# One hybrid decoder layer on one core: another order for the output gates' blocks, and four pieces of side work moved by a step or more

## The chip, the cores and the metric

The kernel runs on one core of a Trainium2 chip. The metric is the device time of one execution in microseconds (us). The kernel before takes 1752.5 us (median of 3 runs, 1751.62 to 1753.2).

## The reference, cut to what matters

```python
h = _rmsnorm(x, norm_gain)                      # x: 256 tokens of 4096 columns, float32
proj = h @ w_in                                 # one combined input projection
(m_q, m_k, m_v, m_o, m_z, m_i, m_f, a_q, ...) = jnp.split(proj, split_points, axis=-1)
qk = jax.nn.silu(_causal_conv(jnp.concatenate([m_q, m_k], axis=-1), w_conv))
...
h_m = _mlstm(mq, mk, mv, i_pre, f_pre)          # 4 heads: scores, decay, numerator / denominator
h_m = jax.nn.sigmoid(m_o) * h_m                 # output gate
h_m = h_m * lax.rsqrt(jnp.mean(h_m * h_m, axis=-1, keepdims=True) + RMS_EPS) * mlstm_norm_gain
y_m = h_m * jax.nn.silu(m_z)                    # second gate
y_a = _nsa(...) * jax.nn.silu(a_z)              # sparse attention, 16 heads
mix = jnp.concatenate([y_m, y_a], axis=-1)
x = x + mix @ w_out
return _rmsnorm(x, final_norm_gain)
```

The change touches the part with the four mLSTM heads and nothing of what is computed.

## The kernel before, in words

**Matmuls.** The weights come as a stream of pairs, each 2 x 128 rows of 512 output columns. A 32-bit product is made of three passes (lines 721 to 723): high half by high half, and each high half by the other's low half. ScalarE (ACT) makes the high half of a pair (line 1253), VectorE (DVE) the low half (line 1775), both three steps ahead of TensorE (PE), in a ring of four slots. A step of the stream is one pair for all 256 tokens: 2 token tiles x 2 x 3 = 12 matmuls.

**Twos.** For some column blocks two blocks are done at once (class `Two`, `two`). Of a pair of blocks some row pairs ("quads") are done in the plain way, one step for each block: an *eight*. The others are done together by a Strassen-like scheme with 7 products in place of 8: a *seven*, which takes the place of two steps and has 21 matmuls. A seven needs sums of weights: DVE makes them in `m_t_raw` (line 2047, then 2052 and 2062), ACT makes their high halves in `m_t_hi` (line 1403 for the first two sums, line 1410 for the other two), DVE their low halves in `m_t_lo` (lines 2057 and 2067). There is one set of these tiles. So the ACT instruction on line 1403 waits for the semaphore `t_used`, which PE raises with the last matmul of the seven before. On PE a seven runs in this order: six matmuls on the plain weights (into `bank_xy` and `acc_a`), six on the first two sums (they wait for `t13_lo`), three on plain weights (into `acc_b`), six on the other two sums (they wait for `t24_lo`, from line 2067).

**Heads.** Each head h of the mLSTM has a block of gates (output gate m_o and second gate m_z as one Two, order `ORDER_M`: 6 sevens and 10 pairs of eights, 32 steps) and, but for the last head, a block of keys (queries and keys of the next head as one column block and its values as the other: 4 sevens, at steps 4, 8, 12 and 16). Heads 0 to 2 run in a hardware loop, and the gates of head 3 stand behind it. They are followed by the first block of the output projection.

**Side work by step.** Each engine's program carries side work by the step's number: scores of the head (`SCORES`), numerators and denominators (`NUMERATOR`, on PE; DVE's `normalise` one step later), sums of the shared and own banks of a Two at its end (`SUMS_GATES`, `shared_products`, `own_products`, lines 2081 and 2087), which free the accumulators `acc_a` and `acc_b` for the next block. In the keys' block: the output gate, the second gate and `head_output` (line 2309) at the three numbers of `PRODUCTS_KEYS`, the scaling of queries and keys on ACT (`key_scale`, line 1612), and at step `CONV_KEYS` PE transposes them (line 763) for the convolution. In the gates of head 3 eight further pieces turn the attention's output into the next left operand: `mix_hi` on ACT (line 1313), `mix_lo` on DVE (line 1845), at the steps of `MIX_TAIL`.

The order within a two is a list of (row pair, block). A Two's `few` says whether a row pair is a quad of the seven kind, `last(h)` in which step block h gets its last product. DVE adds block 0's accumulators when that step's `pe_used` is there.

Of the kernel before, what the change touches and what calls it, by code (L numbers as in the profile page):

```python
# [89 lines left out]
MIX_TAIL, MIX_TURN = 24, 1  # L90
# [10 lines left out]
ORDER_M = (6, 7, 8, 0, 9, 1, 10, 2, 11, 3, 12, 4, 13, 5, 14, 15)  # L101
# [7 lines left out]
def interleaved(order):  # L109

    return tuple((c, h) for c in order for h in range(2))

# [63 lines left out]
PRODUCTS_KEYS, PRODUCTS_LAST = (2, 6, 10), (1, 4, 5)  # L176
SCORES, NUMERATOR = 0, 3
SUMS_GATES, SUMS_KEYS = 28, 18
CONV_V, CONV_KEYS = 1, 22
# [47 lines left out]
def hybrid_layer(nc, x, x_cols_first, w_all, final_norm_gain,  # L227
                 consts, early_consts, toe_bias, s_lo_kept, out):
    ctx = ExitStack()
    with ctx:  # L230
# [208 lines left out]
        def gates_two(h):  # L439

            return Two(4 * h * PAIRS + M0, 2 * h + 1, per_head * h + len(SEVEN), len(SEVEN),
                       interleaved(ORDER_M), (acc[0], acc[1]), [bx, by, bz, bv],
                       (kv_s_hi, m_s_lo), (m_t_hi, m_t_lo, m_t_raw))
# [785 lines left out]
        def _(act):  # L1229
# [319 lines left out]
            def head_pieces(h):  # L1549
# [93 lines left out]
                return two_pieces, conv_at, gates_at, (SUMS_KEYS, key_product), (CONV_KEYS - 1, key_scale)  # L1643
# [24 lines left out]
            gates(HEADS_M - 1, {MIX_TAIL + c: [lambda c=c: mix_hi(c)] for c in range(MIX_M)})  # L1668
# [83 lines left out]
        def _(dve):  # L1752
# [471 lines left out]
            def head_pieces(h):  # L2224
# [72 lines left out]
                def sums_at(w, c, last):  # L2297
                    return (*[(c + part // 2, lambda part=part: shared_products(w, m_shared, part))
                              for part in range(4)], (last, lambda: own_sums(w, 0)))
# [18 lines left out]
                def gates_at(o, z, y):  # L2318
# [6 lines left out]
                              *sums_at(gates_two(h), SUMS_GATES, SUMS_GATES + 3))  # L2325
# [5 lines left out]
            def keys(h):  # L2331
                _, _, gates_at, sums_at, own_sums = head_pieces(h)
                two_stream(keys_two(h), piece_map(
                    *gates_at(*PRODUCTS_KEYS), *sums_at(keys_two(h), SUMS_KEYS, CONV_KEYS - 2),
                    *head_pieces(h + 1)[1](CONV_KEYS)))
                own_sums(keys_two(h), 1)
# [24 lines left out]
            gates(HEADS_M - 1, [(MIX_TAIL + c, lambda c=c: mix_lo(c)) for c in range(MIX_M)])  # L2361
# [234 lines left out]
def weight_stream(w_in, w_out, cmp_k_w1, cmp_v_w1):  # L2596
# [37 lines left out]
    for h in range(HEADS_M):  # L2634
        gates = [block(w_in, run(col + h * BW)) for col in (C_MO, C_MZ)]
        pairs += [gates[i][c] for c, i in interleaved(ORDER_M)]
        if h < HEADS_M - 1:
            blocks = keys(h + 1)
            pairs += [blocks[i][c] for c, i in keys_first(FEW_V)]
# [41 lines left out]
```

## Time and profile before

| | us |
|---|---|
| median of 3 runs | 1752.5 |
| the profiled execution | 1752.96 |
| its span, first to last instruction | 1751.2 |
| PE busy | 1733.5 (99%) |
| DVE busy | 1313.6 (75%) |
| ACT busy | 947.6 (54%) |

In the trace the stretch of the four heads runs from about 788 to 1401 us. Start times are from the span's start. A PE row's duration is that of one matmul through a pipelined array (0.39 us), while the next one starts well before it ends, so idle time in brackets counts only what lies behind that end.

### The profile page before, as it was taken

Reading aid. Unit: us, or ns where it says so; the run is one execution under the profiler, and the core shown is the slowest. Engines: PE = TensorE matmul, PEld = TensorE weight load, DVE = VectorE, ACT = ScalarE, POOL = GpSimd, SP = SyncE. Lnnn points to the kernel's source line nnn. Section 1 sums busy time; section 2 is a strip of 40 time slices with the busy share of each in tenths; the row PEclk is TensorE's granted clock in tenths of the full one; section 3 lists DMA queues with packets and bytes.
Section 4 is the critical chain, followed back from the end, with each engine's and each line's share of the span. In section 5 each row is a group of like instructions: output and inputs, shape, how many; then the busy total and the mean of one; then the engine's idle time right before and its main releaser. Section 6 shows DMA issues by size and latency. Waiting matters only on the chain.

```text
span 1751.2 us, 23455 instructions
## 1 busy us (share of the span) xinstructions
PE 1733.5 (99%) x8000; PEld 1437.0 (82%) x8000; DVE 1313.6 (75%) x1679; ACT 947.6 (54%) x1318; POOL 20.0 (1%) x33
## 2 busy tenths in 40 slices
PE   9999999999999999999999999999999999999997
PEld 7888888888888888888888888888888788888886
DVE  7556786566675756668887888788878988888876
ACT  7535555455555555545555555555555665564553
POOL 0000000000000000000000000000000000000000
PEclk9999999999999999999999999999999999999999
DMA  9657656545455454555646564666565656666674
GB/s 383 241 179 234 214 195 221 185 157 183 154 188 170 158 182 161 174 181 204 216 169 217 205 215 169 217 206 212 174 213 208 206 187 212 216 217 215 217 262 182
DMA packets 98325, 354.59 MB, mean 202 GB/s; under 512 B 10688, under 2 KB 11200, under 8 KB 97472
## 3 DMA queue, kind: packets, MB, share of 16 engines
q1 hardware_dynamic: 94480, 336.96, 55.7%
q10 hardware_dynamic: 3760, 16.52, 2.7%
q8 instruction: 51, 0.84, 0.2%
q14 instruction: 34, 0.28, 0.1%
HBM read 347.67 MB, written 5.77 MB: 202 GB/s over the span
## 4 chain that ended last, share of the span: by engine, by line
PE 88%; DVE 5%; DMA 3%; issue 2%; ACT 1%; SPq 0%; DVEq 0%; POOLq 0%; ACTq 0%; POOL 0%
PE acc_a L721 12%; PE acc_a L723 12%; PE acc_a L722 12%; PE acc_b L721 11%; PE acc_b L723 11%; PE acc_b L722 11%; DMA w_raw<-in_w_all 3%; PE bank_xy L721 3%; PE bank_xy L722 3%; PE bank_xy L723 3%; PE bank_z L723 1%; PE bank_z L721 1%; PE bank_z L722 1%; PE bank_v L722 1%; PE bank_v L723 1%
## 5 line engine op out<-in xcount | busy, mean ns | idle before, releaser
L1775 DVE TENSOR_TENSOR w_split<-w_raw,w_split 128x1024 fp32r<-128x1024 f32 x495 | 599.5, 1222 | 263.0 <-ACT w_split L1253 254.3
L1253 ACT ACTIVATE w_split<-w_raw 128x1024 fp32r<-128x1024 f32 x494 | 518.1, 1056 | 366.1 <-PE acc_b L723 176.8
L721 PE MATMUL acc_a<-w_split,lhs_hi 128*128 128x512 f32 x968 | 379.9, 392 | 2.6 <-DVE stage L2087 2.4
L723 PE MATMUL acc_a<-w_split,lhs_lo 128*128 128x512 f32 x968 | 377.2, 390 | 0.0
L722 PE MATMUL acc_a<-w_split,lhs_hi 128*128 128x512 f32 x968 | 377.2, 390 | 0.0
L721 PE MATMUL acc_b<-w_split,lhs_hi 128*128 128x512 f32 x890 | 348.4, 391 | 0.0
L723 PE MATMUL acc_b<-w_split,lhs_lo 128*128 128x512 f32 x890 | 346.6, 389 | 0.0
L722 PE MATMUL acc_b<-w_split,lhs_hi 128*128 128x512 f32 x890 | 346.5, 389 | 0.0
L721 PEld LDWEIGHTS acc_a<-w_split,lhs_hi 128*128 128x128 f32 x968 | 181.8, 188 | 39.6 <-issue 2.5
L723 PEld LDWEIGHTS acc_a<-w_split,lhs_lo 128*128 128x128 f32 x968 | 181.7, 188 | 38.5
L722 PEld LDWEIGHTS acc_a<-w_split,lhs_hi 128*128 128x128 f32 x968 | 181.9, 188 | 33.8
L723 PEld LDWEIGHTS acc_b<-w_split,lhs_lo 128*128 128x128 f32 x890 | 167.1, 188 | 35.1
L722 PEld LDWEIGHTS acc_b<-w_split,lhs_hi 128*128 128x128 f32 x890 | 167.2, 188 | 33.4
L721 PEld LDWEIGHTS acc_b<-w_split,lhs_hi 128*128 128x128 f32 x890 | 167.1, 188 | 33.2
L2038 DVE TENSOR_TENSOR w_split<-w_raw,w_split 128x1024 fp32r<-128x1024 f32 x120 | 114.2, 951 | 3.5 <-ACT w_split L1397 2.0
L1397 ACT ACTIVATE w_split<-w_raw 128x1024 fp32r<-128x1024 f32 x60 | 63.7, 1062 | 32.7 <-PE acc_a L723 16.7
L1403 ACT ACTIVATE m_t_hi<-m_t_raw 128x1024 fp32r<-128x1024 f32 x36 | 38.2, 1061 | 72.9 <-PE bank_z L723 40.5
L1410 ACT ACTIVATE m_t_hi<-m_t_raw 128x1024 fp32r<-128x1024 f32 x36 | 38.2, 1060 | 56.2 <-DVE m_t_raw L2062 56.2
L2067 DVE TENSOR_TENSOR m_t_lo<-m_t_raw,m_t_hi 128x1024 fp32r<-128x1024 f32 x36 | 44.1, 1226 | 17.9 <-ACT m_t_hi L1410 17.9
L2162 DVE TENSOR_TENSOR pt_lo<-bank_z,pt_hi 128x512 fp32r<-128x512 f32 (+1 forms) x32 | 17.9, 558 | 49.5 <-ACT pct L1487 49.5
L2047 DVE TENSOR_TENSOR m_t_raw<-w_raw 128x1024 f32<-128x1024 f32 x36 | 44.0, 1222 | 11.4 <-DMA w_raw<-in_w_all 7.4
L1485 ACT ACTIVATE pt_hi<-bank_z 128x512 fp32r<-128x512 f32 (+1 forms) x32 | 15.7, 491 | 66.8 <-PE bank_v L1067 66.8
(457 smaller groups left out, 2142.2 us busy)
## 6 DMA issues: line engine op xcount, KB each, us to landing
w_raw<-in_w_all SPq DMA_DIRECT2D x614, 512.0 KB
m_s_lo<-s_lo_kept ACTq DMA_DIRECT2D x4, 1536.0 KB, 7.5
wide<-in_x SPq DMA_DIRECT2D x8, 512.0 KB, 10.3
xres<-in_x ACTq DMA_DIRECT2D x8, 512.0 KB, 5.7
out_y<-wide SPq DMA_DIRECT2D x8, 512.0 KB, 3.6
gained_x<-in_x_cols_first SPq DMA_DIRECT2D x6, 512.0 KB, 7.5
toe<-in_toe_bias ACTq DMA_DIRECT2D x4, 512.0 KB, 5.0
gain_f<-in_final_norm_gain ACTq DMA_DIRECT2D x1, 2048.0 KB, 9.9
```

What stands on the lines that cost most here:

```text
L721: pe.matmul(dst, a[0], b[0], start=start, stop=False)
L722: pe.matmul(dst, a[0], b[1], start=False, stop=False)
L723: return pe.matmul(dst, a[1], b[0], start=False, stop=stop)
L1253: act.activation(w_hi[:, cols], w_raw[:, cols], ACT.Copy).then_inc(hi_done, 1)
L1397: act.activation(w_hi[:, cols], w_raw[:, cols], ACT.Copy).then_inc(hi_done, 1)
L1403: act.activation(sum_hi[:, 0:2 * BW], sum_raw[:, 0:2 * BW], ACT.Copy).then_inc(t13_hi, 1)
L1410: act.activation(sum_hi[:, 2 * BW:].rearrange("p (i c) -> p i c", i=2), sum_raw[:, :].rearrange("p (i c) -> p i c", i=3)[:, 0:3:2, :], ACT ...
L1775: dve.tensor_tensor(w_lo[:, cols], w_raw[:, cols], w_hi[:, cols].bitcast(F32), ALU.subtract).then_inc(lo_done, 1)
L2038: return dve.tensor_tensor(w_lo[:, cols], w_raw[:, cols], w_hi[:, cols].bitcast(F32), ALU.subtract)
L2047: dve.tensor_tensor(sums[:, 0:2, :], tile(1, 0, 2).rearrange("p (i c) -> p i c", i=2), w_raw[:, 2 * s * BW:(2 * s + 4) * BW].rearrange("p ...
L2067: dve.tensor_tensor(sum_lo[:, 2 * BW:].rearrange("p (i c) -> p i c", i=2), sums[:, 0:3:2, :], sum_hi[:, 2 * BW:].bitcast(F32).rearrange("p ...
L2162: dve.tensor_tensor(in_batch(pt_lo, u), transposed_tiles(u), in_batch(pt_hi, u).bitcast(F32), ALU.subtract)
```

## The change

The gates' order `ORDER_M` begins with row pairs 6, 7, 8, 9 (all of them eights), and then 0 and 1 (both sevens) follow each other; 0 stood between 8 and 9 before. A new function, `gates_in_turn`, makes the last two row pairs (14, 15) run for block 0 first and then for block 1, so block 0 (the output gate) gets its last product at step 29 and not 30. Its own sums move from step 31 to 30. The numerators move from step 3 to 4 (and `normalise` with them from 4 to 5). In the keys' block the transposes and the convolution behind them move from 22 to 23, while own sums and key scale stay at 20 and 21; `head_output` moves from step 10 to 15, and DVE waits for it before the shared sums. `MIX_TAIL` spreads the eight mix pieces: steps 24 to 31 before, 10, 14, 18, 22, 26, 28, 31, 31 now.

```diff
@@ -87,7 +87,7 @@
 
 
 MIX_EARLY, MIX_LATE = PAIRS - 2, 11
-MIX_TAIL, MIX_TURN = 24, 1
+MIX_TAIL, MIX_TURN = (10, 14, 18, 22, 26, 28, 31, 31), 1
 
 MIX_M = PAIRS // 2
 
@@ -98,7 +98,7 @@
 TWOS = 3
 SEVEN = tuple(range(6))
 ORDER = (6, 7, 0, 8, 1, 9, 2, 10, 3, 11, 4, 12, 5, 13, 14, 15)
-ORDER_M = (6, 7, 8, 0, 9, 1, 10, 2, 11, 3, 12, 4, 13, 5, 14, 15)
+ORDER_M = (6, 7, 8, 9, 0, 1, 10, 2, 11, 3, 12, 4, 13, 5, 14, 15)
 FEW_V = 4
 S1, S2, S3, S4 = range(4)
 SUM_ORDER, SUMS = (S1, S3, S2, S4), 5
@@ -109,6 +109,12 @@
 def interleaved(order):
 
     return tuple((c, h) for c in order for h in range(2))
+
+
+def gates_in_turn(order):
+
+    last = order[-2:]
+    return interleaved(order[:-2]) + tuple((c, h) for h in range(2) for c in last)
 
 
 def keys_first(quads):
@@ -173,10 +179,11 @@
 
 
 GATES_KEYS, GATES_LAST = (0, 3, 4), (0, 2, 3)
-PRODUCTS_KEYS, PRODUCTS_LAST = (2, 6, 10), (1, 4, 5)
-SCORES, NUMERATOR = 0, 3
+PRODUCTS_KEYS, PRODUCTS_LAST = (2, 6, 15), (1, 4, 5)
+SCORES, NUMERATOR = 0, 4
 SUMS_GATES, SUMS_KEYS = 28, 18
-CONV_V, CONV_KEYS = 1, 22
+CONV_V, CONV_KEYS = 1, 23
+OWN_KEYS = 20
 RESIDUAL = 12
 
 WARM = 8
@@ -439,7 +446,7 @@
         def gates_two(h):
 
             return Two(4 * h * PAIRS + M0, 2 * h + 1, per_head * h + len(SEVEN), len(SEVEN),
-                       interleaved(ORDER_M), (acc[0], acc[1]), [bx, by, bz, bv],
+                       gates_in_turn(ORDER_M), (acc[0], acc[1]), [bx, by, bz, bv],
                        (kv_s_hi, m_s_lo), (m_t_hi, m_t_lo, m_t_raw))
 
         def keys_two(h):
@@ -1640,7 +1647,7 @@
 
                 two_pieces = piece_map((0, values_hi), (SCORES, input_sums_lo), (SCORES + 1, sw_hi_part),
                                        (SUMS_GATES, gate_product))
-                return two_pieces, conv_at, gates_at, (SUMS_KEYS, key_product), (CONV_KEYS - 1, key_scale)
+                return two_pieces, conv_at, gates_at, (SUMS_KEYS, key_product), (OWN_KEYS + 1, key_scale)
 
             def gates(h, late={}, behind=None):
                 found = head_pieces(h)[0]
@@ -1665,7 +1672,7 @@
                 act.wait_ge(s_raw_done, SUM_ORDER.index(f) + 1)
                 act.activation(s_hi[:, f], s_raw[:, f], ACT.Copy).then_inc(s_hi_done, 1)
 
-            gates(HEADS_M - 1, {MIX_TAIL + c: [lambda c=c: mix_hi(c)] for c in range(MIX_M)})
+            gates(HEADS_M - 1, piece_map(*[(MIX_TAIL[c], lambda c=c: mix_hi(c)) for c in range(MIX_M)]))
             last_gates = piece_map(*head_pieces(HEADS_M - 1)[2](*GATES_LAST))
 
 
@@ -2322,7 +2329,7 @@
                 two_pieces = ((SCORES, scores), (SCORES + 1, values_lo), (SCORES + 2, scores_lo),
                               (NUMERATOR + 1, lambda: normalise(0)),
                               (NUMERATOR + 1, lambda: normalise(1)),
-                              *sums_at(gates_two(h), SUMS_GATES, SUMS_GATES + 3))
+                              *sums_at(gates_two(h), SUMS_GATES, SUMS_GATES + 2))
                 return two_pieces, conv_at, gates_at, sums_at, own_sums
 
             def gates(h, late=(), behind=None):
@@ -2331,7 +2338,8 @@
             def keys(h):
                 _, _, gates_at, sums_at, own_sums = head_pieces(h)
                 two_stream(keys_two(h), piece_map(
-                    *gates_at(*PRODUCTS_KEYS), *sums_at(keys_two(h), SUMS_KEYS, CONV_KEYS - 2),
+                    *gates_at(*PRODUCTS_KEYS), (SUMS_KEYS, lambda: dve.wait_ge(ym_done, h + 1)),
+                    *sums_at(keys_two(h), SUMS_KEYS, OWN_KEYS),
                     *head_pieces(h + 1)[1](CONV_KEYS)))
                 own_sums(keys_two(h), 1)
 
@@ -2358,7 +2366,7 @@
                 if f == SUM_ORDER[-1]:
                     last.then_inc(s_lo_done, 1)
 
-            gates(HEADS_M - 1, [(MIX_TAIL + c, lambda c=c: mix_lo(c)) for c in range(MIX_M)])
+            gates(HEADS_M - 1, [(MIX_TAIL[c], lambda c=c: mix_lo(c)) for c in range(MIX_M)])
             late = piece_map(*head_pieces(HEADS_M - 1)[2](*PRODUCTS_LAST))
             for i, f in enumerate(SUM_ORDER):
                 late.setdefault(SUMS + i, []).append(lambda f=f: input_sum(f))
@@ -2633,7 +2641,7 @@
     pairs += sum(keys(0), [])
     for h in range(HEADS_M):
         gates = [block(w_in, run(col + h * BW)) for col in (C_MO, C_MZ)]
-        pairs += [gates[i][c] for c, i in interleaved(ORDER_M)]
+        pairs += [gates[i][c] for c, i in gates_in_turn(ORDER_M)]
         if h < HEADS_M - 1:
             blocks = keys(h + 1)
             pairs += [blocks[i][c] for c, i in keys_first(FEW_V)]
```

Two places of the order. On **ACT**, in the loop's block of gates, the rows from the first seven's second high half (line 1410, in the changed kernel 1417) to the next seven's first (line 1403, then 1410). Before:

```order
L1410 ACTIVATE m_t_hi<-m_t_raw 128x1024 [waits lo_done]
L1247 REGISTER_ALU
L1248 REGISTER_ALU [waits pe_used]
L1253 ACTIVATE w_split<-w_raw 128x1024 [waits w_loaded0]
L1247 REGISTER_ALU
L1253 ACTIVATE w_split<-w_raw 128x1024 [waits w_loaded1,pe_used]
L1397 ACTIVATE w_split<-w_raw 128x1024 [waits w_loaded2,pe_used]
L1398 REGISTER_ALU
L1403 ACTIVATE m_t_hi<-m_t_raw 128x1024 [waits t_used,t13_raw]
```

Now:

```order
L1410 ACTIVATE m_t_hi<-m_t_raw 128x1024 [waits t_used]
L1411 REGISTER_ALU
L1414 ACTIVATE w_split<-w_raw 128x512 [waits w_loaded1,pe_used]
L1416 REGISTER_ALU
L1417 ACTIVATE m_t_hi<-m_t_raw 128x1024 [waits lo_done]
L1401 REGISTER_ALU
L1404 ACTIVATE w_split<-w_raw 128x1024 [waits w_loaded2,pe_used]
L1405 REGISTER_ALU
L1410 ACTIVATE m_t_hi<-m_t_raw 128x1024 [waits t_used,t13_raw]
```

The two plain splits on line 1253 that stood between the sevens are gone from here; the second seven's first high half comes two instructions behind the first seven's last, and still waits for `t_used`.

On **DVE**, in the gates of head 3, the rows from the last shared sum (line 2081, then 2088) to past the own sums of block 0 (line 2087, then 2094). Before:

```order
L2081 TENSOR_TENSOR m_gate<-bank_xy,m_gate 128x512
L1845 TENSOR_TENSOR lhs_lo<-wide,lhs_hi 128x512
L1775 TENSOR_TENSOR w_split<-w_raw,w_split 128x1024
L1845 TENSOR_TENSOR lhs_lo<-wide,lhs_hi 128x512
L1775 TENSOR_TENSOR w_split<-w_raw,w_split 128x1024
L2087 TENSOR_TENSOR stage<-acc_a,stage 128x512 x2
L1845 TENSOR_TENSOR lhs_lo<-wide,lhs_hi 128x512
L1775 TENSOR_TENSOR w_split<-w_raw,w_split 128x1024
```

Now:

```order
L2088 TENSOR_TENSOR m_gate<-bank_xy,m_gate 128x512
L1782 TENSOR_TENSOR w_split<-w_raw,w_split 128x1024
L2094 TENSOR_TENSOR stage<-acc_a,stage 128x512 x2
L1782 TENSOR_TENSOR w_split<-w_raw,w_split 128x1024
L1852 TENSOR_TENSOR lhs_lo<-wide,lhs_hi 128x512 x2
L1782 TENSOR_TENSOR w_split<-w_raw,w_split 128x1024
```

The own sums of block 0 have moved ahead of one plain split (line 1775, then 1782), and two low halves of the mix (line 1845, then 1852) that stood ahead of them now stand behind them or earlier in the block.

## Rows read from the trace of the kernel before

**Rows 1.** The page: busy time (us, share, instructions) and TensorE's granted clock, tenths.

```profile
PE 1733.5 (99%) x8000; PEld 1437.0 (82%) x8000; DVE 1313.6 (75%) x1679; ACT 947.6 (54%) x1318; POOL 20.0 (1%) x33
...
PEclk9999999999999999999999999999999999999999
```

**Rows 2.** Waits of PE over the whole span: us in total, times, longest.

```profile
PE acc_a L721 <- DVE stage L2087: 2.4, 4, 1.6
PE bank_xy L721 <- DVE sw_lo L2262: 1.6, 4, 0.6
...
PE bank_v L763 <- ACT stage L1612: 1.1, 2, 0.6
```

**Rows 3.** Timeline of PE, head 0: start, duration, instruction, [idle before].

```profile
797.29 0.39 PE L723 MATMUL acc_a<-w_split,lhs_lo 128*128 128x512 f32 x1
797.91 0.49 PE L721 MATMUL bank_xy<-mv_hi,sw_hi 128*128 128x512 f32 x1 [0.24 <-DVE sw_lo L2262]
798.24 0.39 PE L722 MATMUL bank_xy<-mv_lo,sw_hi 128*128 128x512 f32 x1
```

**Rows 4.** Timeline of PE, head 0, from a seven's end to the next step.

```profile
844.33 0.39 PE L721 MATMUL acc_a<-w_split,lhs_hi 128*128 128x512 f32 x1
...
847.05 0.39 PE L721 MATMUL acc_b<-w_split,lhs_hi 128*128 128x512 f32 x1
```

**Rows 5.** Timeline of ACT, the same stretch.

```profile
844.59 1.07 ACT L1403 ACTIVATE m_t_hi<-m_t_raw 128x1024 fp32r<-128x1024 f32 x1 [2.39 <-PE bank_z L723]
...
847.67 1.06 ACT L1410 ACTIVATE m_t_hi<-m_t_raw 128x1024 fp32r<-128x1024 f32 x1 [1.50 <-DVE m_t_raw L2062]
```

**Rows 6.** Timeline of DVE, the same stretch, one seven and two eights.

```profile
842.57 1.23 DVE L2047 TENSOR_TENSOR m_t_raw<-w_raw 128x1024 f32<-128x1024 f32 x1 [0.48 <-DMA w_raw<-in_w_all]
...
845.69 1.23 DVE L2057 TENSOR_TENSOR m_t_lo<-m_t_raw,m_t_hi 128x1024 fp32r<-128x1024 f32 x1
846.95 0.69 DVE L2062 TENSOR_TENSOR m_t_raw<-w_raw,m_t_raw 128x512 f32<-128x512 f32 x1
...
848.77 1.23 DVE L2067 TENSOR_TENSOR m_t_lo<-m_t_raw,m_t_hi 128x1024 fp32r<-128x1024 f32 x1 [0.53 <-ACT m_t_hi L1410]
849.91 2.38 DVE L1775 TENSOR_TENSOR w_split<-w_raw,w_split 128x1024 fp32r<-128x1024 f32 x2
```

**Rows 7.** Timeline of DVE, head 0, first and last row of normalise.

```profile
806.49 0.15 DVE L2269 COPY den<-bank_v 128x2 f32<-128x2 f32 x1
...
808.02 0.74 DVE L2275 TENSOR_SCALAR hm<-bank_z,den 128x512 f32<-128x512 f32 x1
```

**Rows 8.** Timeline of DVE, keys behind head 0.

```profile
909.75 1.41 DVE L2309 SCALAR_TENSOR_TENSOR wide<-hm,hr,m_gate 128x512 f32 x2
911.08 2.35 DVE L1775 TENSOR_TENSOR w_split<-w_raw,w_split 128x1024 fp32r<-128x1024 f32 x2
```

**Rows 9.** Timeline of PE, the same stretch.

```profile
912.05 0.39 PE L723 MATMUL bank_z<-m_t_hi,m_s_lo 128*128 128x512 f32 x1
912.35 0.50 PE L721 MATMUL acc_a<-w_split,lhs_hi 128*128 128x512 f32 x1
```

**Rows 10.** Timeline of DVE, end of the gates of head 0.

```profile
874.18 1.23 DVE L1775 TENSOR_TENSOR w_split<-w_raw,w_split 128x1024 fp32r<-128x1024 f32 x1 [1.50 <-ACT w_split L1253]
875.32 1.28 DVE L2087 TENSOR_TENSOR stage<-acc_a,stage 128x512 f32<-128x512 f32 x2
```

**Rows 11.** Timeline of ACT, keys behind head 0, the key scale.

```profile
932.45 1.34 ACT L1612 ACTIVATE stage<-stage,rstd 128x512 f32<-128x512 f32 x2 [0.26 <-DVE stage L2087]
```

**Rows 12.** Timeline of PE, start of the output projection.

```profile
1400.92 0.47 PE L721 MATMUL acc_a<-w_split,lhs_hi 128*128 128x512 f32 x1 [1.56 <-DVE stage L2087]
```

**Rows 13.** Timeline of DVE, end of the gates of head 3.

```profile
1398.36 0.68 DVE L1845 TENSOR_TENSOR lhs_lo<-wide,lhs_hi 128x512 fp32r<-128x512 f32 x1
```

**Rows 14.** Timeline of DVE, gates of head 3, a wait for weights.

```profile
1351.16 0.69 DVE L2038 TENSOR_TENSOR w_split<-w_raw,w_split 128x512 fp32r<-128x512 f32 x1
...
1356.89 1.22 DVE L2047 TENSOR_TENSOR m_t_raw<-w_raw 128x1024 f32<-128x1024 f32 x1 [1.02 <-issue]
```

## The prediction
> **What bounds the kernel now.** I read the page first: PE is busy 1733.5 of 1751.2 us, 99%, and its granted clock shows 9 tenths or more in all 40 slices [rows 1]. So PE is the bound, and a change of order can only move the short stretches in which PE waits. The steps of PE give the scale: one plain step of 12 matmuls runs from 844.33 to 847.05, 2.72 us, one matmul every 0.227 us [rows 4]. A seven has 21 matmuls, 4.76 us.
>
> The second view was the list of PE's waits [rows 2]. Its idle time counts from a matmul's modelled end, 0.39 us after its start, while the next one normally starts after 0.227. So each wait costs its idle time and 0.16 us. Head 0 shows it: starts at 797.29 and 797.91, 0.62 us apart with 0.24 us in brackets, so 0.40 us are lost. The next matmul comes at 798.24, 0.33 later and not 0.227: a start after a wait costs 0.10 us more [rows 3].
>
> The third view was the timeline of the three engines around each of those waits and through one seven with its two plain steps [rows 4 to 6].
>
> **What goes.** Four waits, all in the heads' stretch.
>
> (1) Numerators wait for `sw_lo`: 1.6 us in 4 waits [rows 2], with 4 x 0.16 and 4 x 0.10 that is 2.6 us. One step later PE comes 2.72 us later than the longest of them (0.6 us of idle time) needs. All 2.6 us go.
>
> (2) Start of a keys' block (3 times) and of the output projection (once): 2.4 us in 4 waits for the own sums, the last one 1.56 [rows 2, 12]. With 4 x 0.16 and 4 x 0.10: 3.4 us. Before, the own sums start at 875.32, right behind the split of step 34 (874.18), which itself idled 1.50 us for ACT [rows 10]. They now stand ahead of that split and wait only for step 29, which is two steps old. They can run in that idle time and end about 1.7 us before PE needs the banks. In head 3 the eight low halves of the mix (0.68 us each [rows 13]) no longer crowd in there either. All 3.4 us go.
>
> (3) Transposes of the keys wait for ACT's key scale: 1.1 us in 2 waits [rows 2], and a third, shorter one that the list does not name. With 0.16 each I take 1.6 us. The scale's two rows end at 932.45 + 1.34 = 933.79 [rows 11], 0.4 us before PE's transposes. Own sums and scale stay at their steps and PE comes a step, 2.72 us, later. All of it goes, with over 2 us to spare.
>
> (4) In a keys' block `head_output`, 1.41 us, stands ahead of the split that PE needs next: the split (1.22 us from 911.08) ends at 912.30, PE starts at 912.35, 0.30 after its last matmul [rows 8, 9]. With the slow restart 0.18 us, 3 times: 0.5 us. At step 15 the piece stands behind the last seven, where DVE has 2.72 us for each 1.22 us split. The added wait on `ym_done` is for DVE's own product: queued behind it are the shared sums, and it costs the latency of one result.
>
> Sum of gains: 2.6 + 3.4 + 1.6 + 0.5 = 8.1 us.
>
> **What comes: two sevens side by side.** Today no matmul of a seven waits. But ACT's first high half does: at 844.59 it ends an idle time of 2.39 us, released by PE's last matmul of the seven before [rows 5], since there is one set of sum tiles. PE's next step had begun at 844.33, which I call E. From there the chain is fixed:
> - ACT line 1403 starts at E + 0.26 [rows 4, 5];
> - DVE line 2057 runs from 845.69 and ends at 846.92, E + 2.59 [rows 6];
> - line 2062 and then ACT line 1410 follow (847.67 to 848.73), and DVE line 2067 ends at 848.77 + 1.23 = 850.00, E + 5.67 [rows 5, 6].
>
> Before, two plain steps of 5.44 us lie between E and the next seven, which needs the first pair of sums 1.36 us after its start (E + 6.80) and the second 3.40 us after it (E + 8.84). Both are there. With two sevens side by side the second starts at E. It does its six plain matmuls and needs the first sums at E + 1.36, but has them at E + 2.69 (0.10 us for the signal). With the slow restart, nine matmuls end at E + 4.83. It needs the second sums then and gets them at E + 5.77. Six matmuls and the restart: it ends at E + 7.24. Without waiting it would end at E + 4.76. Loss 2.48 us, in each of four gates' blocks: 9.9 us. No other work fills this time, since PE's program is in order.
>
> **Is the second seven's other work ready?** Between the two sevens DVE now does normalise, 806.49 to 808.76, 2.27 us [rows 7], then the second seven's raw sums. The first seven sits two plain steps later than before, so DVE's part of it ends about 1.3 us before PE reaches it. Normalise then ends about 0.5 us before PE needs `hm_done`, and the raw sums and first low half fit with some 0.9 us. I cost this at nothing; if that cover fails, a few tenths per head.
>
> **Behind the pair.** The next seven's raw sums need the weights of two steps, fetched once the slots are free, that is after the split on line 2038. In head 3 that split ends at 1351.85 and the raw sums start at 1356.89: 5.04 us, the last 1.02 idle [rows 14]. In head 0 the idle time is 0.48 [rows 6], so the wait is about 4.5 us. From the raw sums to the end of line 2067 it is 7.4 us (842.57 to 850.00). The split ends at E + 3.9 in the pair's second seven, so the second low halves of the next seven are there at E + 3.9 + 4.5 + 7.4 = E + 15.8; PE needs them at E + 7.24 + 5.44 + 3.40 = E + 16.08. With 5.04 us they are 0.3 us late. From there on a cycle needs 5.6 + 4.5 = 10.1 us on this chain (weights, sums, splits) against PE's 10.20: it holds. With 5.04 it needs 10.6 and loses 0.4 us in each of the three cycles left. Before, DVE entered these cycles with a lead of 2 to 3 us, and the drift was hidden; the pair uses that lead up. So a block loses between nothing and 0.3 + 3 x 0.4 + four restarts = 1.9 us more. I take 1.2 us in all, nearly all in head 3, where the 5.04 was seen; the bounds are 0 and 7.6. The mix pieces in head 3 fall into DVE's idle time before the raw sums if the wait is there.
>
> **Sum.** -8.1 + 9.9 + 1.2 = +3.0 us. The profiled execution took 1752.96 us (span 1751.2 and 1.8 around it), so 1755.9 for that one; against the median of 1752.5 I forecast 1755.3, taking 0.2 us off for small gains not listed.
>
> **Two rules of the Trainium skill.** PE never idles at a seven today, while ACT waits for the one tile set [rows 5]. The Trainium skill, page Perfetto Trace Analysis, section Optimization Strategy, says that a gap which repeats on the engine that should be saturated can mean too few buffers. By today's PE rows alone the pair would be free (-6.9 us in all); by the rule it is the 9.9 us gap. The chain above bears the rule out.
>
> The granted clock stayed at its upper level, 2.4 GHz, through the longest wait, 1.56 us [rows 1, 12]. The page TensorE: Matmul & The Clock Gate of the Trainium skill, Part 1, says that a TensorE that idles falls to half the clock. The trace shows no fall after a wait of that length, and the pair's waits are 1.3 and 0.9 us.
>
> **The rivals.**
> - *A, the forecast:* pair loses 2.5 us a head, gains real, little drift. 1750.5 to 1756.0, chance 0.51 with what lies within 0.2%.
> - *B, slower:* the same, but the drift behind the pair appears in more than one head. It decides once the weights take over 4.76 us (E + 16.08 less 7.4 and 3.9). All four heads: -8.1 + 9.9 + 7.6 = +9.4, 1761.9; two heads: about 1758. For it: 1.02 us of idle time before the raw sums in head 3. Against: 0.48 in head 0. Chance 0.34.
> - *C, faster:* the pair costs little, because the second sums, or both, are ready in a way that I overlook. With only the first wait (1.3 + 0.1 a head) -8.1 + 5.7 = -2.4; with none -8.1, 1744.4. Against it: `t_used` still stands before the second seven's first high half. Chance 0.13, for what ends more than 3.5 us below; the -2.4 would still lie within.
> - *D:* the clock falls in the pair's waits. A step at half clock takes 2.72 us more; four steps a head would be +43 us. Against it: rows 1. Chance 0.01.
> - *E, the change does not do what it says:* normalise, now squeezed between sevens, delays PE at `hm_done` by more than 0.5 us a head; +2 us on top of A, about 1757. Chance 0.01.
>
> **Chances and range.** A measurement tells about 0.2% apart, 3.5 us. Faster than that: C, 0.13. Within: 0.51. Slower: B, D, E, 0.36. The range for 8 in 10 leaves out the better part of C and the far end of B: 1750.0 to 1760.0.
>
> **What would show it.** In the changed profile: the waits for `sw_lo`, for the own sums on line 2094 and for line 1619's scale gone; in each gates' block a wait of PE for `m_t_lo` of line 2064 with idle time about 1.2 us and one for line 2074 of 0.8. Rows of line 2074 ending later than 3.4 us after a seven's start would be B. I am wrong at the root if PE runs the second seven of the pair in 4.8 us.

## The result and the profile after

| | before | after |
|---|---|---|
| median | 1751.93 us (1751.23 to 1755.08, 19 runs) | 1755.12 us (1754.54 to 1756.44, 19 runs) |
| the profiled execution | 1752.96 | 1755.31 |
| its span | 1751.2 | 1753.5 |

The ratio is 1.0017, with a 95% interval of 1.001 to 1.0024. The change costs 3.2 us by the medians and 2.3 us by the two profiled executions; the forecast was 1755.3.

The page of the changed kernel, busy time and granted clock. It answers to [rows 1].

```profile
PE 1734.4 (99%) x8000; PEld 1437.5 (82%) x8000; DVE 1311.5 (75%) x1679; ACT 945.0 (54%) x1318; POOL 20.1 (1%) x33
...
PEclk9999999999999999999999999999999999999999
```

The work is the same and the clock is the same. What differs is where PE waits. The list of PE's waits in the changed kernel (us in total, times, longest), which answers to [rows 2]. All lines of the kernel have moved down by 7.

```profile
PE bank_xy L728 <- DVE m_t_lo L2064: 4.4, 4, 1.1
PE acc_a L728 <- DVE m_t_lo L2074: 3.1, 5, 0.7
```

The waits for `sw_lo`, for the own sums and for the key scale are gone, and two waits for sum tiles stand in their place. PE around the second seven of the pair in head 0 (start, duration, instruction, idle before):

```profile
818.62 0.39 PE L728 MATMUL bank_xy<-w_split,lhs_hi 128*128 128x512 f32 x1
...
819.75 0.39 PE L730 MATMUL acc_a<-w_split,lhs_lo 128*128 128x512 f32 x1
821.25 0.50 PE L728 MATMUL bank_xy<-m_t_hi,in_s_hi 128*128 128x512 f32 x1 [1.11 <-DVE m_t_lo L2064]
821.60 0.40 PE L729 MATMUL bank_xy<-m_t_lo,in_s_hi 128*128 128x512 f32 x1
...
823.23 0.39 PE L730 MATMUL acc_b<-w_split,m_s_lo 128*128 128x512 f32 x1
824.34 0.50 PE L728 MATMUL acc_a<-m_t_hi,lhs_hi 128*128 128x512 f32 x1 [0.72 <-DVE m_t_lo L2074]
...
825.83 0.39 PE L728 MATMUL acc_a<-w_split,lhs_hi 128*128 128x512 f32 x1
```

The second seven starts at 818.62 (the E of the prediction) and the step behind it at 825.83: 7.21 us for 21 matmuls, where 21 x 0.227 is 4.76. ACT and DVE in the same stretch, first ACT, the rows that answer to [rows 5]:

```profile
818.88 1.06 ACT L1410 ACTIVATE m_t_hi<-m_t_raw 128x1024 fp32r<-128x1024 f32 x1 [6.47 <-PE bank_z L730]
...
821.96 1.06 ACT L1417 ACTIVATE m_t_hi<-m_t_raw 128x1024 fp32r<-128x1024 f32 x1 [1.50 <-DVE m_t_raw L2069]
```

and DVE, the rows that answer to [rows 6]:

```profile
814.62 1.22 DVE L2054 TENSOR_TENSOR m_t_raw<-w_raw 128x1024 f32<-128x1024 f32 x1
815.87 0.69 DVE L2059 TENSOR_TENSOR m_t_raw<-m_t_raw,w_raw 128x512 f32<-128x512 f32 x1
...
819.97 1.23 DVE L2064 TENSOR_TENSOR m_t_lo<-m_t_raw,m_t_hi 128x1024 fp32r<-128x1024 f32 x1 [2.27 <-ACT m_t_hi L1410]
821.23 0.69 DVE L2069 TENSOR_TENSOR m_t_raw<-w_raw,m_t_raw 128x512 f32<-128x512 f32 x1
...
823.05 1.23 DVE L2074 TENSOR_TENSOR m_t_lo<-m_t_raw,m_t_hi 128x1024 fp32r<-128x1024 f32 x1 [0.53 <-ACT m_t_hi L1417]
```

Read the brackets as a relay. ACT idled 6.47 us until PE's last matmul on the old sums (818.39). The new raw sums had ended at 815.87 + 0.69 = 816.56, over 2 us before ACT's start, so what ACT still lacked was the tile and not its input. DVE idled 2.27 us for ACT, and then PE idled 1.11 us for DVE. Every link is an engine that was idle just before: none is short of time, each waits for the one set of tiles. What a second set would give back is not shown: no run has one.

Lost time is counted below as the time between two starts of PE beyond the usual 0.227 us. Added up over the two traces, in us:

| where | before | after |
|---|---|---|
| numerators, 4 heads | 2.68 | 0 |
| start of the keys' blocks, 3 | 1.70 | 0 |
| start of the output projection | 1.80 | 0 |
| transposes, 3 | 1.70 | 0 |
| keys' block, step 14, 3 | 0.60 | 0 |
| keys' block, step 10, 3 | 0 | 0.68 |
| second seven of the pair, 4 x 2.38 | 0 | 9.51 |
| the sevens behind the pair | 0 | 0.68 |
| sum | 8.5 | 10.9 |

The difference, 2.4 us, is that of the two spans (2.3) to a tenth.

### The profile page after: what moved, and what is told of

The parts are those of the page before. It is cut to its first block, busy times and chain, and to the rows that moved or that the text cites. A ratio compares the mean times of both kernels' runs of the same rounds, so it can differ in the third digit from the quotient of the medians.

```text
span 1753.5 us, 23452 instructions
## 1 busy us (share of the span) xinstructions
PE 1734.4 (99%) x8000; PEld 1437.5 (82%) x8000; DVE 1311.5 (75%) x1679; ACT 945.0 (54%) x1318; POOL 20.1 (1%) x33
## 3 DMA queue, kind: packets, MB, share of 16 engines
HBM read 347.67 MB, written 5.77 MB: 202 GB/s over the span
## 4 chain that ended last, share of the span: by engine, by line
PE 97%; DVE 1%; ACT 1%; DMA 0%; issue 0%; DVEq 0%; POOLq 0%; POOL 0%; ACTq 0%; SPq 0%
PE acc_a L728 13%; PE acc_a L730 13%; PE acc_a L729 13%; PE acc_b L728 12%; PE acc_b L730 12%; PE acc_b L729 12%; PE bank_xy L730 3%; PE bank_xy L729 3%; PE bank_xy L728 3%; PE bank_z L730 1%; PE bank_z L728 1%; PE bank_z L729 1%; PE bank_v L729 1%; PE bank_v L730 1%; PE bank_v L728 1%; PE bank_z L1072 1%
## 5 line engine op out<-in xcount | busy, mean ns | idle before, releaser
L2074 DVE TENSOR_TENSOR m_t_lo<-m_t_raw,m_t_hi 128x1024 fp32r<-128x1024 f32 x36 | 44.1, 1226 | 18.9 <-ACT m_t_hi L1417 18.9
L2064 DVE TENSOR_TENSOR m_t_lo<-m_t_raw,m_t_hi 128x1024 fp32r<-128x1024 f32 x36 | 43.9, 1219 | 9.2 <-ACT m_t_hi L1410 9.2
## 6 DMA issues: line engine op xcount, KB each, us to landing
wide<-in_x SPq DMA_DIRECT2D x8, 512.0 KB, 10.6
```

Of the source, the lines that this page charges most:

```text
L2064: dve.tensor_tensor(sum_lo[:, 0:2 * BW], sum_raw[:, 0:2 * BW], sum_hi[:, 0:2 * BW].bitcast(F32), ALU.subtract).then_inc(t13_lo, 1)
L2074: dve.tensor_tensor(sum_lo[:, 2 * BW:].rearrange("p (i c) -> p i c", i=2), sums[:, 0:3:2, :], sum_hi[:, 2 * BW:].bitcast(F32).rearrange("p ...
```

## The experiments

Two theories are told apart. Theory 1: each wait of PE has its own cause, and the pair's is the one set of sum tiles. Theory 2: VectorE is late in general, so that time gained at one place comes back as a wait at another. Ratios are against the kernel before, run beside each kernel. The median of before was 1751.9 to 1752.3 us in these comparisons.

| kernel | median us | ratio, 95% interval | span |
|---|---|---|---|
| after | 1755.12 | 1.0017 (1.001 to 1.0024) | 1753.5 |
| x1_apart | 1750.25 | 0.9989 (0.998 to 0.9998) | 1748.4 |
| x2_pair_only | 1762.8 | 1.006 (1.0046 to 1.0074) | 1760.8 |
| x3_ends_first | 1751.28 | 0.9996 (0.9987 to 1.0005) | 1749.5 |
| x4_pair_late | 1761.94 | 1.0054 (1.004 to 1.0068) | 1760.8 |
| x5_two_pairs | 1765.16 | 1.0075 (1.0061 to 1.0089) | 1762.8 |
| x6_output_at_10 | 1756.92 | 1.0027 (1.0016 to 1.0038) | 1755.1 |
| x8_mix_crowded | 1755.41 | 1.0018 (1.0009 to 1.0027) | 1753.9 |
| x9_apart_at_3 | 1745.14 | 0.9961 (0.9947 to 0.9974) | 1743.0 |
| x10_gate_7 | 1744.32 | 0.9957 (0.9943 to 0.9971) | 1742.6 |
| x11_sw_lo_early | 1749.39 | 0.9984 (0.9975 to 0.9993) | 1747.4 |
| x12_transposes_23 | 1750.8 | 0.9992 (0.9982 to 1.0001) | 1749.0 |

**The pair alone (x2_pair_only).** The kernel before with the new order of quads and nothing else.

```diff
-ORDER_M = (6, 7, 8, 0, 9, 1, 10, 2, 11, 3, 12, 4, 13, 5, 14, 15)
+ORDER_M = (6, 7, 8, 9, 0, 1, 10, 2, 11, 3, 12, 4, 13, 5, 14, 15)
```

> The kernel before with nothing but the new order of row pairs (6, 7, 8, 9, 0, 1, ...): numerators stay at step 3. Theory 1: the full price of the pair without any of the gains, 4 x 2.4 = +9.5 us, and up to 1.5 us of drift behind it in head 3: +9.5 to +11, about 1762. Theory 2: with normalise one step earlier VectorE has over 2.7 us more before the second seven, so at least half of the waits go: +5 or less.

Measured: +10.6 us. PE's waits in this kernel:

```profile
PE bank_xy L721 <- DVE m_t_lo L2057: 4.4, 4, 1.1
PE acc_a L721 <- DVE m_t_lo L2067: 2.9, 4, 0.7
PE acc_a L721 <- DVE stage L2087: 2.0, 4, 1.1
PE bank_xy L721 <- DVE sw_lo L2262: 1.6, 4, 0.6
```

By the spans it is +9.6. The pair's waits are those of the changed kernel to a tenth (the fifth wait of its 3.1 us, 0.17, stood behind the pair), and the old waits stand beside them: the pair pays for none of them. By starts, the pair loses 2.38 us a head here as well, 9.5 in all.

**The same pair elsewhere (x4_pair_late).** Sevens 4 and 5 side by side at steps 22 to 25, with no normalise and, but for the mix pieces of head 3, no other side work beside them.

```diff
-ORDER_M = (6, 7, 8, 0, 9, 1, 10, 2, 11, 3, 12, 4, 13, 5, 14, 15)
+ORDER_M = (6, 7, 8, 0, 9, 1, 10, 2, 11, 3, 12, 4, 5, 13, 14, 15)
```

> The kernel before with the pair at another place: row pairs 4 and 5 side by side near the end of the gates' block (steps 22 to 25), where VectorE has no normalise and, but for head 3, no other piece between them. Theory 1: the same chain over the same tiles, 2.4 us a head, +9.5 us, first wait 1.27 and second 0.88 us beyond the normal distance. Theory 2: nothing, or at most 1 us a head.

Measured: +9.7 us (9.6 by the spans), with PE's starts again 1.27 and 0.88 us late (plus 0.11 twice) in each head. So neither normalise nor the place makes the price.

**Two pairs (x5_two_pairs).** The changed kernel with sevens 2 and 3 side by side too.

```diff
-ORDER_M = (6, 7, 8, 9, 0, 1, 10, 2, 11, 3, 12, 4, 13, 5, 14, 15)
+ORDER_M = (6, 7, 8, 9, 0, 1, 10, 11, 2, 3, 12, 4, 13, 5, 14, 15)
```

> The changed kernel with a second pair (row pairs 2 and 3 side by side behind two plain pairs 10 and 11): the suspected cost doubled. Theory 1: another 4 x 2.4 = 9.5 us on the changed kernel, about +12.7 us against before, less the 0.2 to 0.4 us of drift it now shows. Theory 2: the second pair has no normalise in it and four plain steps ahead of it, so below +2 us on the changed kernel.

Measured: 10.0 us over the changed kernel in medians, 9.3 in spans; one more pair, one more price, 9.3 by the starts (four times 2.3). PE's waits:

```profile
PE acc_a L728 <- DVE m_t_lo L2074: 5.8, 8, 0.7
PE bank_xy L728 <- DVE m_t_lo L2064: 5.7, 7, 1.1
PE bank_xy L728 <- DVE w_split L2045: 1.8, 3, 0.8
```

The second pair shows the drift as well: PE is late for the plain split (line 2045) at the start of its second seven, since that split stands on DVE behind the raw sums, and waits less for the first low half then. The starts are 0.30, 0.60, 0.69 and 1.00 us late in heads 0 to 3; the first is too short for the list. The sum per pair stays at 2.3 to 2.4 us.

**Pair undone (x1_apart).** The changed kernel with the old order of quads, and normalise at step 4.

```diff
-ORDER_M = (6, 7, 8, 9, 0, 1, 10, 2, 11, 3, 12, 4, 13, 5, 14, 15)
+ORDER_M = (6, 7, 8, 0, 9, 1, 10, 2, 11, 3, 12, 4, 13, 5, 14, 15)
...
-                              (NUMERATOR + 1, lambda: normalise(0)),
-                              (NUMERATOR + 1, lambda: normalise(1)),
+                              (NUMERATOR, lambda: normalise(0)),
+                              (NUMERATOR, lambda: normalise(1)),
```

> The changed kernel with its sevens apart again (row pair 0 between 8 and 9, as before) and normalise in the numerators' step; all else of the change stays. Theory 1, the one set of sum tiles makes the second seven of the pair wait: the 2.4 us a head of the changed trace (1.27 + 0.88 and two slow restarts) go, 9.5 us in all, and PE's four old waits stay away; against the kernel before -8.5 + 0.7 = about -8 us, 1744. Theory 2, the rival: VectorE is simply behind in the gates' blocks, whatever the order of the sevens (normalise and mix pieces among them), and the waits come back elsewhere: near the changed kernel, +3 us.

Measured: -2.0 us, a miss of 6. The pair's waits are gone, and a new one has come. The three engines in head 0, from this kernel's trace, first PE:

```profile
811.44 0.47 PE L728 MATMUL bank_xy<-m_t_hi,in_s_hi 128*128 128x512 f32 x1 [1.08 <-DVE hm L2282]
```

ACT:

```profile
803.60 1.06 ACT L1410 ACTIVATE m_t_hi<-m_t_raw 128x1024 fp32r<-128x1024 f32 x1 [4.39 <-PE bank_v L1154]
```

DVE:

```profile
804.69 1.23 DVE L2064 TENSOR_TENSOR m_t_lo<-m_t_raw,m_t_hi 128x1024 fp32r<-128x1024 f32 x1 [3.25 <-ACT m_t_hi L1410]
...
807.77 1.23 DVE L2074 TENSOR_TENSOR m_t_lo<-m_t_raw,m_t_hi 128x1024 fp32r<-128x1024 f32 x1 [0.53 <-ACT m_t_hi L1417]
...
810.46 0.74 DVE L2282 TENSOR_SCALAR hm<-bank_z,den 128x512 f32<-128x512 f32 x1
```

Follow it backwards. PE's first seven overwrites `bank_xy`, so it waits until normalise is through with the banks (its last row ends at 810.46 + 0.74). Normalise stands behind DVE's work for that seven, which waits for ACT's high half. And ACT waits 4.39 us for line 1154, the last matmul of the numerators: the sum tile `m_t_hi` lies in the same memory as the numerators' operands `mv_hi` and `mv_lo`. I had not seen this. With the numerators at step 4 and the first seven at step 6, that chain is too long by 1.3 us in three heads and 1.0 in the last, 5.0 in all by starts. So the two parts of the change belong together. The numerators at step 4 need the first seven later, and four quads of eights ahead of it are what puts it at step 8.

**The other way out (x9_apart_at_3).** The old order of quads, the numerators back at step 3, and `sw_lo` made one step earlier, ahead of `values_lo`. All else as in the changed kernel.

```diff
-ORDER_M = (6, 7, 8, 9, 0, 1, 10, 2, 11, 3, 12, 4, 13, 5, 14, 15)
+ORDER_M = (6, 7, 8, 0, 9, 1, 10, 2, 11, 3, 12, 4, 13, 5, 14, 15)
...
-SCORES, NUMERATOR = 0, 4
+SCORES, NUMERATOR = 0, 3
...
-                two_pieces = ((SCORES, scores), (SCORES + 1, values_lo), (SCORES + 2, scores_lo),
+                two_pieces = ((SCORES, scores), (SCORES + 1, scores_lo), (SCORES + 1, values_lo),
```

> The sevens apart again, the numerators at step 3 as before (with them at 4 the first seven at step 6 waits for the numerators' end through ScalarE and for normalise, 1.3 us a head), and the low half of the scores made ahead of the values' low half in VectorE's piece of step 1, so that it is there 1 us earlier; all other parts as in the change. Theory 1: no pair (-9.5 on the changed kernel), drift behind it gone (-0.7), all four old waits gone but step 10's 0.7 us: about -7.8 us against before, 1744. Theory 2 (VectorE is the limit in the gates, gains at one place come back at another): the numerators' wait or a seven's stays and less than half of that is seen.

Measured: -7.1 us against before (-7.8 expected), -10 against the changed kernel. ACT and then DVE in head 0, the same chain:

```profile
800.62 1.06 ACT L1410 ACTIVATE m_t_hi<-m_t_raw 128x1024 fp32r<-128x1024 f32 x1 [1.67 <-PE bank_v L1154]
```

```profile
807.63 0.74 DVE L2282 TENSOR_SCALAR hm<-bank_z,den 128x512 f32<-128x512 f32 x1
```

The high half still waits for line 1154, but 2.98 us earlier than in x1_apart, and normalise ends 2.83 us earlier; PE does not wait.

**`sw_lo` alone (x11_sw_lo_early).** The kernel before with only that line.

```diff
-                two_pieces = ((SCORES, scores), (SCORES + 1, values_lo), (SCORES + 2, scores_lo),
+                two_pieces = ((SCORES, scores), (SCORES + 1, scores_lo), (SCORES + 1, values_lo),
```

> The kernel before with one edit: at step 1 of a gates' block VectorE makes the low half of the scores (sw_lo) ahead of the values' (values_lo), where it was a step behind them. Theory 1 (each wait of PE has its own cause, and goes with it): the four numerators' waits, 2.68 us in all, go, nothing comes; about 1749.6 us against 1752.2, 2.6 less. Theory 2 (VectorE is late in general, and what is gained at one place comes back as a wait at the next): less than 1.3 us of gain, with waits of PE grown at the first seven, at step 14 of a keys' block or at the own sums.

Measured: -2.9 us, and no wait for `sw_lo` left. PE's waits in the heads:

```profile
PE acc_a L721 <- DVE stage L2087: 1.3, 4, 0.4
PE bank_v L763 <- ACT stage L1612: 1.2, 2, 0.6
```

Theory 1 holds here. The wait for the own sums reads 1.3 and not 2.4 us as in [rows 2]: the one at the start of the output projection is 0.39 us, where the profiled execution of before had 1.56 [rows 12]. The transposes' wait did not shrink: 1.9 us by the starts, where before had 1.7.

**Transposes alone (x12_transposes_23).** The kernel before with the transposes and the convolution at 23.

```diff
-CONV_V, CONV_KEYS = 1, 22
+CONV_V, CONV_KEYS = 1, 23
+OWN_KEYS = 20
...
-                return two_pieces, conv_at, gates_at, (SUMS_KEYS, key_product), (CONV_KEYS - 1, key_scale)
+                return two_pieces, conv_at, gates_at, (SUMS_KEYS, key_product), (OWN_KEYS + 1, key_scale)
...
-                    *gates_at(*PRODUCTS_KEYS), *sums_at(keys_two(h), SUMS_KEYS, CONV_KEYS - 2),
+                    *gates_at(*PRODUCTS_KEYS), *sums_at(keys_two(h), SUMS_KEYS, OWN_KEYS),
```

> The kernel before with one edit: in the keys' block the transposes and the convolution stand at step 23 in place of 22, own sums and key scale stay at 20 and 21; head_output stays at step 10. Theory 1: the transposes' waits, 1.70 us in three, go, nothing comes; about 1750.5 us against 1752.2, a ratio of 0.9990. Theory 2 (VectorE's convolution, now a step later, is late at the next block's start): the numerators' waits or the first seven of the next gates' block grow by as much, ratio 1.000 or above.

Measured: -1.3 us (ratio 0.9992, interval 0.9982 to 1.0001), and no wait for the key scale. What is queued behind it, `sw_lo` of the next head, is 0.2 us worse in all (1.8 against 1.6, longest 0.7 against 0.6). Most of the gain stays, in line with theory 1, though the interval touches no change.

**The ends alone (x3_ends_first).** The kernel before with `gates_in_turn` and the own sums one step earlier.

```diff
+def gates_in_turn(order):
+    last = order[-2:]
+    return interleaved(order[:-2]) + tuple((c, h) for h in range(2) for c in last)
...
-                       interleaved(ORDER_M), (acc[0], acc[1]), [bx, by, bz, bv],
+                       gates_in_turn(ORDER_M), (acc[0], acc[1]), [bx, by, bz, bv],
...
-                              *sums_at(gates_two(h), SUMS_GATES, SUMS_GATES + 3))
+                              *sums_at(gates_two(h), SUMS_GATES, SUMS_GATES + 2))
...
-        pairs += [gates[i][c] for c, i in interleaved(ORDER_M)]
+        pairs += [gates[i][c] for c, i in gates_in_turn(ORDER_M)]
```

> The kernel before with nothing but the output gate's block ending first (row pairs 14 and 15 for block 0, then for block 1) and its own sums one step earlier. Theory 1, each of PE's old waits stands alone and goes with its own part: the three waits at a keys' start (0.57 us each with the slow restart) go, 1.7 us; in head 3 the mix pieces still crowd VectorE, but one step earlier: of 1.8 us between 0.5 and 1.8 go. -2.2 to -3.5 us in all, and the numerators', transposes' and step 14's waits stay as they were. Theory 2, the waits are one lateness handed on, and what goes at one place comes at the next: within 1 us of before.

Measured: -0.9 us (1.7 by the spans), interval across no change. Theory 1 asked for 2.2 to 3.5: a miss. All four waits for the own sums are gone (3.5 us by starts). But in the keys' block, `head_output` is now in the way. PE at step 14, behind head 0:

```profile
912.64 0.50 PE L727 MATMUL acc_a<-w_split,lhs_hi 128*128 128x512 f32 x1 [0.32 <-DVE w_split L1781]
```

There PE loses 0.59 us in each keys' block, where it lost 0.2 before, and 0.22 at step 10, where it lost nothing: 1.8 us come back. So theory 2 is partly right, inside one block: a PE that starts the block 0.57 us earlier meets the same DVE queue. Part (2) of the change needs part (4).

**`head_output` back at 10 (x6_output_at_10).**

```diff
-PRODUCTS_KEYS, PRODUCTS_LAST = (2, 6, 15), (1, 4, 5)
+PRODUCTS_KEYS, PRODUCTS_LAST = (2, 6, 10), (1, 4, 5)
```

> The changed kernel with head_output back at step 10 of the keys' block. The changed trace shows a small wait at step 10 (0.22 us a head) in place of the one at step 14. Theory 1, the second gate's 1.22 us piece ahead of step 10's split makes it, and head_output's place is good for step 14's: both waits stand now, +0.6 us or more, as the output piece comes 0.6 us of lead too late. Theory 2, only one lateness exists and it shows at one place: 0.

Measured: 1.8 us over the changed kernel, 1.6 by the spans. PE at step 14 in this kernel:

```profile
914.42 0.50 PE L728 MATMUL acc_a<-w_split,lhs_hi 128*128 128x512 f32 x1 [0.31 <-DVE w_split L1782]
```

It waits as in x3_ends_first: 0.58 us, three times. With the other parts in place, moving `head_output` is worth 1.6 to 1.8 us and not 0.5.

**The mix pieces (x8_mix_crowded).** The changed kernel with the mix pieces back at steps 24 to 31.

```diff
-MIX_TAIL, MIX_TURN = (10, 14, 18, 22, 26, 28, 31, 31), 1
+MIX_TAIL, MIX_TURN = (24, 25, 26, 27, 28, 29, 30, 31), 1
```

> The changed kernel with the eight mix pieces at steps 24 to 31 again. Theory 1 (the wait at the start of the output block goes because the own sums come earlier, whatever the mix pieces do): same time as the changed kernel, 1755.1 us against 1752.2 of the kernel before, and no wait for line 2094 in the trace. If the spread of the mix pieces mattered, up to 1.8 us more, with a wait of PE for the own sums at the start of the output projection. If the pieces at steps 10 to 22 cost something at the pair's drift in head 3, up to 0.5 us less.

Measured: +0.3 us against the changed kernel, spans 0.4 apart, within what can be told. No wait at the output projection's start came back. The spread is worth nothing that can be told here. Inside the heads this trace is 0.7 us shorter than the changed kernel's, since no seven behind the pair waits in it, and it is 1.1 us longer ahead of them, where the edit changes nothing. Whether the spread has a part in the 0.44 us that head 3 of the changed kernel loses behind the pair, one trace cannot tell.

**The last wait (x10_gate_7).** x9_apart_at_3 with the second gate at step 7 of the keys' block.

```diff
-PRODUCTS_KEYS, PRODUCTS_LAST = (2, 6, 15), (1, 4, 5)
+PRODUCTS_KEYS, PRODUCTS_LAST = (2, 7, 15), (1, 4, 5)
```

> The kernel of x9 with the second gate's piece on VectorE one step later in the keys' block (7, behind the split of step 10, and not 6, ahead of it). Theory 1: the wait at step 10 goes, another 0.6 us: about -8.4 us against before, 1743.5, and no wait of TensorE is left in the heads' stretch. Theory 2: ScalarE's or VectorE's later piece moves the wait to the next seven: 0 or slower than x9.

Measured: 1744.32 us, 0.8 below x9_apart_at_3 (0.4 by the spans). It beats both kernels: 7.9 us under before, 10.8 under the changed one. From the first head to the end PE now has no start that is more than 0.1 us late. DVE in the keys behind head 0:

```profile
899.07 1.22 DVE L1782 TENSOR_TENSOR w_split<-w_raw,w_split 128x1024 fp32r<-128x1024 f32 x1
900.20 1.22 DVE L1828 SCALAR_TENSOR_TENSOR m_gate<-stage,m_gate 128x1024 f32<-128x1024 f32 x1
901.34 1.22 DVE L1782 TENSOR_TENSOR w_split<-w_raw,w_split 128x1024 fp32r<-128x1024 f32 x1
```

The gate's product (line 1828) now stands behind the split that PE needs first.

## Why the prediction was right, step by step

**The sum** was +3.0 us; the medians give +3.2 and the profiled executions +2.3. The mechanism was right: the four waits went from their places, and the pair's two waits came within 0.06 us of the times that were forecast. That the number came so close is in part luck. By the starts the pair was taken 0.4 us and the drift 0.5 us too dear, which offset the 0.6 us that term (4) is short. The forecast also started from a median of 1752.5 us where 19 runs give 1751.93, and the 0.2 us that it took off for small gains not listed shows in no trace.

**(1) Numerators, 2.6 us: right.** 2.68 by the starts, all gone. x11_sw_lo_early takes the same wait away by itself and gains 2.9.

**(2) Starts of the blocks, 3.4 us: right in the two traces (3.5), mis-sized for other runs.** The own sums now run at 874.54, and PE's first matmul into `acc_a` comes without a wait. DVE, and below it PE, in the changed kernel; they answer to [rows 10]:

```profile
873.40 1.22 DVE L1782 TENSOR_TENSOR w_split<-w_raw,w_split 128x1024 fp32r<-128x1024 f32 x1
874.54 1.28 DVE L2094 TENSOR_TENSOR stage<-acc_a,stage 128x512 f32<-128x512 f32 x2
876.08 1.23 DVE L1782 TENSOR_TENSOR w_split<-w_raw,w_split 128x1024 fp32r<-128x1024 f32 x1 [0.26 <-ACT w_split L1260]
```

```profile
877.28 0.39 PE L730 MATMUL acc_b<-w_split,lhs_lo 128*128 128x512 f32 x1
877.51 0.39 PE L728 MATMUL acc_a<-w_split,lhs_hi 128*128 128x512 f32 x1
```

They end 1.69 us ahead of PE, as worked out (1.7). But 1.56 us of the waiting was one row [rows 12], at the output projection. The same wait is 0.39, 0.38 and 0.39 in x11_sw_lo_early, x12_transposes_23 and x4_pair_late, and 1.12 in x2_pair_only, which leave that place alone. So its size varies between executions, and the term is worth 1.2 us less in three of these four. That would explain why the medians differ by 3.2 where the two traces differ by 2.3; it was not tested by more profiles of the kernel before. My second reason, that the mix's low halves no longer crowd there, carried nothing: with the own sums earlier, x8_mix_crowded keeps the crowd and has no wait.

**(3) Transposes, 1.6 us: right.** 1.70 by the starts, all gone; alone they gave 1.3.

**(4) `head_output`, 0.5 us: right at its place, wrong in the sum.** Step 14's 0.6 us went, and 0.68 came at step 10, which I had not looked at. DVE and then PE in the changed kernel:

```profile
901.05 1.22 DVE L1828 SCALAR_TENSOR_TENSOR m_gate<-stage,m_gate 128x1024 f32<-128x1024 f32 x1
902.19 2.35 DVE L1782 TENSOR_TENSOR w_split<-w_raw,w_split 128x1024 fp32r<-128x1024 f32 x2
```

```profile
903.12 0.39 PE L730 MATMUL bank_z<-m_t_hi,m_s_lo 128*128 128x512 f32 x1
903.46 0.50 PE L728 MATMUL acc_a<-w_split,lhs_hi 128*128 128x512 f32 x1
```

The split's first half ends at 903.41 and PE starts at 903.46, 0.34 after its last matmul. I asked of (2) only whether its own wait goes, not who is met by a PE that comes earlier. That lead of 0.57 us also made step 14 worth more: 1.6 to 1.8 us by x6_output_at_10. In the sum this term is 0.6 us short.

**The pair, 9.9 us: right.** Forecast E + 2.69, E + 5.77 and E + 7.24; measured E + 2.63, E + 5.72 and E + 7.21. The loss is 2.38 us by the starts where I had 2.48, and alone it is +10.6 and +9.7 us in two places. PE's rows of before show no gap at a seven, ACT's do [rows 5], and PE got one as soon as nothing stood between the sevens. By the rule that I weighed (the Trainium skill, page Perfetto Trace Analysis, section Optimization Strategy) such a gap can mean too few buffers; the traces agree, but the rule asks for it on the engine to be saturated, where it could not be seen beforehand.

**The drift, 1.2 us, bounds 0 and 7.6: 0.7, mis-sized.** The last row of it in the changed kernel, PE in head 3:

```profile
1360.39 0.50 PE L728 MATMUL acc_a<-m_t_hi,lhs_hi 128*128 128x512 f32 x1 [0.17 <-DVE m_t_lo L2074]
```

It appears at the first seven behind the pair, as said, in heads 1 (0.24 us) and 3 (0.44), and not again: the 0.4 us for each later cycle did not come. The next raw sums (line 2054) start at E + 8.45, 8.83, 8.16 and 9.04 in heads 0 to 3 of this trace, and only the two latest cost something. With the same pair they start at E + 7.9 to 8.2 in x2_pair_only and x8_mix_crowded, and there the drift is nothing. In x6_output_at_10 only one later seven of head 3 loses 0.33. So it is no fixed cost of the pair; it hangs on when DVE can start on the next weights. That this is a wait for the weights themselves is read from the head 0 row of [rows 6]; the 1.02 us of [rows 14] stands as "issue", a wait whose releaser the profile does not show.

**The rivals.** B (slower by the drift) fell: 0.7 us and not 7.6. Its mechanism exists; two pairs bring it out in all four heads, and even there the price per pair stays near 2.4. C (faster) fell: both waits of the pair came in every head of every kernel with one pair. D (the clock) fell: all slices at 9, with eight waits of 0.7 to 1.1 us more, and right behind them PE's starts are 0.23 us apart again (821.84, 822.07, 822.30). The rule that I weighed there (the Trainium skill, page TensorE: Matmul & The Clock Gate, Part 1) has no case in any run here; the longest wait in the traces is 1.7 us. E (normalise squeezed) fell for this kernel, but it is what happens in x1_apart, where it costs 5.0 us. The half microsecond to spare that I worked out for this kernel was there. Normalise's last row on DVE, and the matmul of PE that needs it:

```profile
813.97 0.74 DVE L2282 TENSOR_SCALAR hm<-bank_z,den 128x512 f32<-128x512 f32 x1
```

```profile
815.22 0.39 PE L728 MATMUL bank_xy<-m_t_hi,in_s_hi 128*128 128x512 f32 x1
```

The first ends at 814.71, 0.51 us ahead.

## What to carry to other kernels

Before two users of a single-buffered tile are put side by side, look at the engine that refills it, not at the one that is to be saturated: if its idle time ahead of the refill ends with the last user, a price is waiting to be paid. That idle time is the sign and not the size (it was 2.39 us before and 6.47 in the changed kernel). The size is the chain of refill less the work that the last engine can still do meanwhile. Here the two legs of the chain took 2.6 and 3.1 us, PE had six and nine matmuls for them, and it cost the same 2.4 us wherever the pair stood.

A gain that makes the bound engine earlier shifts it against every queue of side work downstream. Walk those queues once more with the new lead, and test edits both alone and together: the ends alone gave 0.9 us of 3.5 (1.7 by the spans), and `head_output` moved beside them was worth 1.6 to 1.8 us, not 0.5. Look also at what shares memory: `m_t_hi` on top of the numerators' operands tied two parts of the change together that looked separate, and a smaller edit (make `sw_lo` earlier) avoided both the wait and the pair.

## What the runs showed of the hardware

- A matmul that starts after a wait delays the next by 0.07 to 0.12 us beyond the usual 0.227 us, after waits of any length seen (0.1 to 1.7 us). It is a part of the price of each wait that does not grow with it, 1.4 us in the 13 waits of the changed kernel.
- A wait can be absent from the list of waits and still cost: at 903.46 PE is 0.11 us late and the next start 0.11 more, and the row has no bracket, because the new start lies within the modelled duration of the last matmul.
- TensorE's granted clock stayed at its upper level, 2.4 GHz, in all 40 slices, with PE idle 1.1 and then 0.7 us in each head, the ends of the two waits 3.1 us apart.
